# Encoder layer: the last K group of the first projection pass split in two, small loads placed behind the pass

## What is computed

```python
mod = silu(c) @ w_mod + b_mod            # 2048 -> 6 * 2048
sh1, sc1, gt1, sh2, sc2, gt2 = split(mod, 6)
h = x * (1 + sc1) + sh1
proj = h @ w_in                          # columns of four mixers: A (RWKV-7), B, C, D
y = concat(mixers(proj))
x = layer_norm(ALPHA * x + (1 + gt1) * (y @ w_out))
h = x * (1 + sc2) + sh2
gate, up = split(h @ w_up, 2)
x = layer_norm(ALPHA * x + (1 + gt2) * ((silu(causal_dwconv(gate)) * up) @ w_down))
```

## Time and profile before

| | us |
|---|---|
| median of 3 runs | 1441.3 (1440.76 to 1445.62) |
| profiled execution | 1437.06 |
| its span, first to last instruction | 1435.1 |
| PE busy | 1342.1 (94%) |
| DVE busy | 975.2 (68%) |
| ACT busy | 538.9 (38%) |
| POOL busy | 158.9 (11%) |
| DMA, mean over the span | 222 GB/s |

### The profile page before, as it was taken

The page is one execution under the profiler, slowest core; times in us unless marked ns, Lnnn a source line. Parts: engine busy times, 40 slices in busy tenths (PEclk is TensorE's granted clock), DMA queues, the critical chain, the costliest instruction groups (busy, mean ns, idle before and its releaser), DMA issues.

```text
span 1435.1 us, 23097 instructions
## 1 busy us (share of the span) xinstructions
PE 1342.1 (94%) x8833; PEld 1219.4 (85%) x8833; DVE 975.2 (68%) x1266; ACT 538.9 (38%) x765; POOL 158.9 (11%) x223
## 2 busy tenths in 40 slices
PE   1988899999999999997999999999999999999994
PEld 1777798989787777787999999999999998888883
DVE  5776787787779877568877787546555654545545
ACT  1000533343433435334544344434444453333331
POOL 4332111100001111001710100000000000000001
PEclk9899989999999999998999999999999999999997
...
DMA packets 142879, 318.98 MB, mean 222 GB/s; under 512 B 12142, under 2 KB 19680, under 8 KB 141792
## 3 DMA queue, kind: packets, MB, share of 16 engines
...
HBM read 315.98 MB, written 2.10 MB: 222 GB/s over the span
## 4 chain that ended last, share of the span: by engine, by line
PE 73%; DVE 14%; DMA 8%; issue 2%; ACT 2%; POOL 0%; DVEq 0%; POOLq 0%; ACTq 0%; SPq 0%
PE G L1377 64%; PE M L1377 8%; DMA MODA<-in_w_mod_dram 6%; DVE ACC L836 5%; DVE WLO L816 2%; DMA RAW<-in_w_out_dram 1%; DMA RAW<-in_w_in_dram 1%; ACT WHI L521 1%; DMA MODR<-in_w_mod_dram 1%; PE M L1538 0%; DVE X L1361 0%; DVE X L1370 0%; DVE SM L1125 0%; DVE HLO L868 0%; PE M L1640 0%
## 5 line engine op out<-in xcount | busy, mean ns | idle before, releaser
L1377 PE MATMUL G<-HHI,WHI 128*128 128x256 f32 (+1 forms) x1744 | 503.1, 288 | 0.0
L1377 PE MATMUL G<-HLO,WHI 128*128 128x256 f32 (+1 forms) x1744 | 495.4, 284 | 0.0
L1377 PE MATMUL G<-HHI,WLO 128*128 128x256 f32 (+1 forms) x1744 | 495.4, 284 | 0.0
L1377 PEld LDWEIGHTS G<-HHI,WHI 128*128 128x128 f32 (+1 forms) x1744 | 335.7, 192 | 4.2 <-issue 3.7
L1377 PEld LDWEIGHTS G<-HLO,WHI 128*128 128x128 f32 (+1 forms) x1744 | 335.8, 193 | 0.5 <-issue 0.5
L1377 PEld LDWEIGHTS G<-HHI,WLO 128*128 128x128 f32 (+1 forms) x1744 | 335.5, 192 | 0.0
L816 DVE TENSOR_TENSOR WLO<-RAW,WHI 128x1024 fp32r<-128x1024 f32 x182 | 221.3, 1223 | 167.4 <-ACT WHI L521 164.0
L821 DVE TENSOR_TENSOR WLO<-RAW,WHI 128x1024 fp32r<-128x1024 f32 x174 | 217.6, 1271 | 140.5 <-ACT WHI L527 140.3
L521 ACT ACTIVATE WHI<-RAW 128x1024 fp32r<-128x1024 f32 x182 | 191.9, 1059 | 209.9 <-PE G L1377 176.8
L527 ACT ACTIVATE WHI<-RAW 128x1024 fp32r<-128x1024 f32 x174 | 180.0, 1055 | 185.7 <-PE G L1377 138.0
L836 DVE SCALAR_TENSOR_TENSOR ACC<-MODR,SM,ACC 128x1024 f32<-128x1024 f32 x118 | 150.8, 1278 | 15.6 <-DMA MODR<-in_w_mod_dram 13.0
...
## 6 DMA issues: line engine op xcount, KB each, us to landing
RAW<-in_w_up_dram SPq DMA_DIRECT2D x176, 512.0 KB, 4.5
MODR<-in_w_mod_dram POOLq DMA_DIRECT2D x160, 512.0 KB, 5.6
RAW<-in_w_in_dram SPq DMA_DIRECT2D x88, 512.0 KB, 5.7
RAW<-in_w_down_dram SPq DMA_DIRECT2D x88, 512.0 KB, 4.3
MODA<-in_w_mod_dram POOLq DMA_DIRECT2D x32, 512.0 KB, 13.8
RAW<-in_w_out_dram SPq DMA_DIRECT2D x32, 512.0 KB, 4.5
...
```

What stands on the lines that cost most here:

```text
L1377: return pe.matmul(out_, l, r, start=start, stop=stop, skip_group_check=True)
```

## The change

- The last group (chunks 21 to 27, K tiles 12 to 15) is reordered: K, R and V chunks of tiles 12 and 13, then the LORA chunk of all four, then K, R, V of tiles 14 and 15. A LORA half waits only for the tiles of h that it reads.
- Its modulation, q = 48 to 63, comes in two half parts of 8 tiles: the first 8 hold the columns of K tiles 12 and 13, the others those of 14 and 15. A tile keeps its 512 KB but now has 2 rows of `w_mod` by 2 x 256 columns. It is loaded by two DMAs with rows of 1 KB (before: one DMA, rows of 2 KB), and added by two DVE instructions of 512 columns that wait for each other, instead of one of 1024.
- PE's column sums for the first half part (4 products) stand ahead of chunk 19, those of the second between the halves of chunk 22. Before, the 8 products stood ahead of chunk 21.
- The five small loads and `LNAB` stand between the loads of chunks 27 and 28.
- `DONE_IN` and `SETUP` follow: the LORA block is done first, then K, R, V. Tanh and sigmoid become a step "gates" of their own at place 26; squares, norms and the reciprocals stand 3 places later or more. Indices of semaphores move by one (`mod_sum`, `mod_col`).

```diff
@@ def chunk_at(n):
+    if g == GROUPS - 1:
+        return [(K_BLOCK, 12, 2), (R_BLOCK, 12, 2), (V_BLOCK, 12, 2), (LORA, 12, 4),
+                (K_BLOCK, 14, 2), (R_BLOCK, 14, 2), (V_BLOCK, 14, 2)][i]
...
-DONE_IN = {23: K_BLOCK, 24: LORA, 26: R_BLOCK, 28: V_BLOCK, 32: QI_BLOCK} | \
+DONE_IN = {25: LORA, 26: K_BLOCK, 27: R_BLOCK, 28: V_BLOCK, 32: QI_BLOCK} | \
...
+GROUP_AT = [(0, 0), (7, 0), (14, 0), (19, 0), (22, 1)]
+GROUP_KT = [(0, 4), (4, 8), (8, 12), (12, 14), (14, 16)]
+GROUP_MODS = [16, 32, 48, 56, 64]
...
-SETUP = {(23, 1): "squares", (24, 1): "norms", (25, 0): "inverse 0", (25, 1): "inverse 1", (26, 1): "inverse 2",
-         (27, 1): "inverse 3", (29, 1): "lora", (30, 1): "cumulate", (31, 1): "hats"}
+SETUP = {(26, 0): "gates", (26, 1): "squares", (27, 1): "norms", (28, 0): "inverse 0", (28, 1): "inverse 1", (29, 0): "inverse 2",
+         (30, 0): "inverse 3", (29, 1): "lora", (30, 1): "cumulate", (31, 1): "hats"}
@@ SP
-                if n == FIRST_CHUNKS + 3:
+                if n == WHOLE:
                     sp.dma_start(CBT[:, :], const_b.bitcast(bf16)).then_inc(late_in, 16)
...
-                if n == FIRST_CHUNKS + 5:
                     sp.wait_ge(h_lo, KT)
                     sp.dma_start(LNAB[:, :], rwkv_ln_b[0, :].partition_broadcast(P)).then_inc(lnab_in, 16)
@@ POOL
+                if m == 3:
+                    half, pair_ = divmod(t, KT // 2)
+                    c0 = m * 512 + half * 256
+                    for s_ in range(2):
+                        pool.dma_start(buf.rearrange("p (k s n) -> p k s n", k=2, s=2)[:, :, s_, :],
+                                       wm6[:, 2 * pair_:2 * pair_ + 2, s_, c0:c0 + 256]).then_inc(mod_in[s], 16)
+                    continue
@@ DVE, mod_add
+                if m == GROUPS - 1:
+                    half, pair_ = divmod(t, KT // 2)
+                    a = a[:, half * 512:half * 512 + 512]
+                    for k in range(2):
+                        ck, wk = CC[:, 2 * pair_ + k:2 * pair_ + k + 1], w[:, k * 512:k * 512 + 512]
+                        if pair_ == 0 and k == 0:
+                            mark(dve.tensor_scalar(a, wk, ck, None, ALU.mult))
+                            continue
+                        if k == 0:
+                            dve.wait_ge(mod_done, q)
+                        else:
+                            settle()
+                        ins = dve.scalar_tensor_tensor(a, wk, ck, a, ALU.mult, ALU.add)
+                        mark(ins) if k == 0 else ins.then_inc(mod_done, 1)
+                    return
@@ DVE, the groups
-            for g in range(GROUPS):
-                mod_add(g + 1, 0)
+            for g, kts in enumerate(GROUP_KT):
+                q = GROUP_MODS[g]
+                mod_add(*divmod(q, KT))
                 mod_cols(g)
                 dve.wait_ge(mod_col, g + 1)
-                for kt in range(4 * g, 4 * g + 4):
+                for kt in range(*kts):
                     h_new_tile(kt)
...
@@ PE
+                    q0 = 4 if GROUP_MODS[g] % KT == 0 and g == len(GROUP_KT) - 1 else 0
+                    mod_reduce(min(g, GROUPS - 1), range(q0, q0 + 2 * (GROUP_KT[g][1] - GROUP_KT[g][0])))
...
+                if n < WHOLE and (half == 0 or kts == 4):
+                    pe.wait_ge(h_new, kt + (kts if kts == 2 else 2 * half + 2))
...
-                if n <= FIRST_CHUNKS and n % GROUP_CHUNKS == 0:
-                    first_parts((n // GROUP_CHUNKS,))
                 for half in range(2):
+                    if (n, half) in GROUP_AT:
+                        first_parts((GROUP_AT.index((n, half)),))
                     w_in_half(n, half)
```

More of the change, by code:

```diff
@@ L44 @@
 MODS_IN = (MOD_PARTS - 2) * KT
-MOD_LAPS = 4 * KT // FIRST_RING + (MODS_IN - 4 * KT) // RING
+MOD_LAPS = 5 * KT // FIRST_RING + (MODS_IN - 4 * KT) // RING
 UP_MODS = 4
@@ L578, in setup @@
             def setup(what):
-                if what == "lora":
+                if what == "gates":
                     act.wait_ge(evac_lora, 2)
@@ L583, in setup @@
                     act.activation(PA[:, 13, :], PA[:, 13, :], ACT.Sigmoid)
+                elif what == "lora":
                     act.wait_ge(lora_pe, 2)
@@ L829, in mod_add @@
                 a, ck = ACC[:, m % 2, :], CC[:, t:t + 1]
+                if t == 0 and m >= 2:
+                    dve.wait_ge(mod_sum, m - 1 if m <= GROUPS else m)
+                if m == GROUPS - 1:
[13 more added lines that the diff above has]
+                    return
                 if t == 0:
-                    if m >= 2:
-                        dve.wait_ge(mod_sum, m - 1)
                     ins = dve.tensor_scalar(a, w, ck, None, ALU.mult)
@@ L839, in mod_cols @@
             def mod_cols(m):
-                dve.wait_ge(mod_sum, m + 1)
-                if m < GROUPS:
-                    two = lambda a: a[:, 0:32].rearrange("p (s k) -> p s k", s=2)[:, :, 4 * m:4 * m + 4]
-                    dve.tensor_tensor(two(MC), M[3][:, 0:8].rearrange("p (s k) -> p s k", s=2), two(BMC), ALU.add)\
+                if m < len(GROUP_KT):
+                    k0, k1 = GROUP_KT[m]
+                    dve.wait_ge(mod_sum, m + 1)
+                    two = lambda a: a[:, 0:32].rearrange("p (s k) -> p s k", s=2)[:, :, k0:k1]
+                    dve.tensor_tensor(two(MC), M[3][:, 0:2 * (k1 - k0)].rearrange("p (s k) -> p s k", s=2), two(BMC), ALU.add)\
                        .then_inc(mod_col, 1)
                     return
+                m -= 1
+                dve.wait_ge(mod_sum, m + 2)
                 at = slice(8 * m + 16, 8 * m + 24)
@@ L876, in h_new_tile @@
                                   MC[:, SH1 + kt:SH1 + kt + 1], ALU.mult, ALU.add).then_inc(h_new, 1)
-            for g in range(GROUPS):
-                mod_add(g + 1, 0)
+            for g, kts in enumerate(GROUP_KT):
+                q = GROUP_MODS[g]
+                mod_add(*divmod(q, KT))
                 mod_cols(g)
                 dve.wait_ge(mod_col, g + 1)
-                for kt in range(4 * g, 4 * g + 4):
+                for kt in range(*kts):
                     h_new_tile(kt)
-                mod_add(g + 1, 1)
-                for kt in range(4 * g, 4 * g + 4):
+                mod_add(*divmod(q + 1, KT))
+                for kt in range(*kts):
                     h_split(kt, 0)
-                if g == 0:
-                    for n in range(AHEAD):
-                        split_lo(n)
-                if g < GROUPS - 1:
-                    for t in range(MODS_BESIDE_H, KT):
-                        mod_add(g + 1, t)
-                        if t % 2:
-                            split_lo(g * GROUP_CHUNKS + t // 2 - 1 + AHEAD)
+                if g + 1 < len(GROUP_KT):
+                    for q in range(q + MODS_BESIDE_H, GROUP_MODS[g + 1]):
+                        mod_add(*divmod(q, KT))
             def evac_in(b):
@@ L1167, in _ @@
                     if last_turn is not None:
-                        mod_cols(last_turn)
+                        mod_cols(last_turn + 1)
                     last_turn = turns.get((n, half))
@@ L1397, in tm, with mod_reduce @@
                 return ins
-            def mod_reduce(m):
-                for q in range(8):
-                    ins = mm(M[3][:, q:q + 1], ACC[:, m % 2, q * P:(q + 1) * P], ONES[:, 0:1],
+            def mod_reduce(m, qs=range(8)):
+                for q in qs:
+                    ins = mm(M[3][:, q - qs[0]:q - qs[0] + 1], ACC[:, m % 2, q * P:(q + 1) * P], ONES[:, 0:1],
                              start=True, stop=True)
@@ L1420, in first_parts @@
             def first_parts(ms):
-                for m in ms:
-                    pe.wait_ge(mod_done, (m + 1) * KT)
-                    if m:
-                        pe.wait_ge(mod_col, m)
-                    mod_reduce(m)
+                for g in ms:
+                    pe.wait_ge(mod_done, GROUP_MODS[g])
+                    if g:
+                        pe.wait_ge(mod_col, g)
+                    q0 = 4 if GROUP_MODS[g] % KT == 0 and g == len(GROUP_KT) - 1 else 0
+                    mod_reduce(min(g, GROUPS - 1), range(q0, q0 + 2 * (GROUP_KT[g][1] - GROUP_KT[g][0])))
             def w_in_half(n, half):
@@ L1487, in setup @@
                 elif what == "norms":
-                    pe.wait_ge(mod_col, 4)
+                    pe.wait_ge(mod_col, len(GROUP_KT))
                     pe.wait_ge(evac_lora, 2)
```

12 lines of the change are left out of this document (6 added, 6 removed).

## The result

The change takes 1448.1 us (median of 20 runs, 1443.37 to 1456.24), the kernel before 1442.7 us (median of 20, beside them): a ratio of 1.0037, 95% interval 1.0021 to 1.0053, or **+3.0 to +7.6 us, 5.4 in the middle**. That is measurably slower, and under the 0.5% that the prediction took as its bound. One of the twenty executions of the kernel before took 6478 us and is left out of the ratio and its interval. 1448.9 was predicted, with 1440 to 1455 as the range. The profiled execution of the change took 1447.8 us (span 1445.9); that of before took 1437.06 (span 1435.1), 5.6 us under the median of its own 20 runs, so the difference of these two spans (10.8 us) is twice that of the medians. In what follows the traces give places and causes, and the ratios give the time.

A forecast was written before the change was run, and what follows sets the result against it. Up to about 159 us arriving weights and modulation were the bound, then DVE until "gram". 2.9 + 4.3 + 0.4 = +7.6 us on 1437.06 gave 1444.7; with the median 4.2 above, 1448.9, range 1440 to 1455.

The forecast's parts named there:

- The first pass: PE up to chunk 24: no stall worth counting, chunk 24 ends at 145.4, chunk 28 issued 7 us earlier.
- Chunk 28's landing: SP's queue: chunk 28 waits behind the small loads, lands at 161 (151.2 to 165.5); DVE splits it 2.9 us later.
- Behind the split: DVE from chunk 28's split to "gram": moved work adds 4.3 us, R's evacuation waiting for ACT adds 0.4.
- From "gram" to the end: After "gram" PE is the bound again and carries the +7.6 us to the end as it is.
- Rows of 1 KB: Loads of tiles 48 to 63: 12% more engine time per MB, 2.6 us, covered, so nothing booked.
- In time: Rival, chance 0.22: chunk 28 lands by 157 as DVE's additions stall for their tiles; -2.2 to +3 us.
- Starved modulation: Rival, chance 0.15: narrow rows cut POOL's share per queue turn, last tile lands at 134 to 136; +9 to +13 us.
- PE sets the pace: Rival, chance 0.08: "gram" waits for PE, DVE's work can come later; needs chunk 28 by 152; -8 us.
- the prize: PE in the first pass, around chunks 19 to 22: 5.1 us of idle time and 2.2 us of low clock.
- the moved work: K's evacuation, two norm steps and one reciprocal, now behind DVE's split of chunk 28: +4.3 us.

The follow-up runs named there:

- e2: The change with all six small loads ahead of chunk 32, behind the loads of 28 to 31; ratio to the kernel before 0.9993.
- e7: The kernel before with modulation tiles 48 to 63 loaded by two DMAs each with rows of 1 KB; ratio to the kernel before 1.0018.

## Why the prediction was right, and where not

The mechanism was right: the first pass gained what was forecast, chunk 28 queued behind the small loads, and DVE passed the delay on to "gram". That 1448.9 lies within 0.8 us of the measured 1448.1 is partly luck, as two errors of the sum made up for each other.

- **The first pass: right.** Chunk 24 was to end at 145.4 and ended at 145.0, chunk 28's issue was to come at 145.8 and came at 145.52. PE had no idle time over 0.4 us between 103 and 155 us. 1.54 us for a tile in two additions (1.5 estimated) and 1.05 us for the half sums (1.0) were right.
- **Chunk 28's landing: right in its cause, 1.7 us short.** 161 predicted, 162.7 measured. Two things were mis-sized. From 141.9 to 162.7 us SP's queue moved 4.00 MB, where I had 3.1 (I had counted a rest of 0.1 MB and nothing of the chunks issued behind 28; but chunk 26, 0.52 MB, issued at 138.18, landed only 8.0 us later), and POOL's 3.65 (3.9). And the rate was not the earlier trace rows's 0.388 MB per us throughout, but 0.367 on the whole, with the slump of the last section in it. The change's queues in that stretch (packets, MB, share of 16 engines), and its windows around the slump (columns of the earlier trace rows):

```profile
q1 hardware_dynamic: 2416, 4.00, 55.7%
q0 software_dynamic: 1005, 3.65, 48.5%
```

```profile
146.00:148.00 2.00, 2.00 (x11) 1.77 (x10) 1.08 (x2) 0.00 (x0) 0.53 (x1) 1.00 1.02 410
...
150.00:152.00 2.00, 2.00 (x11) 1.75 (x10) 0.61 (x1) 0.00 (x0) 0.11 (x1) 1.00 1.02 318
```

- **Behind the split: right in its cause, 1.5 us too much.** 4.3 + 0.4 was booked, 3.2 measured: DVE is busy 3.6 us longer there (four reciprocals instead of three, K's evacuation and the norm steps, with 14 additions at 17.5 us instead of 17.8), has 0.4 us less idle time, and R's evacuation waits only 0.2. The two errors made up for each other: the sum was 7.6 at "gram" and the trace shows 7.8. In e2 this step takes 4.5 us. The early tanh and sigmoid save one table load, not two: sigmoid's table is loaded again for the gates, at 176.49 in the change; DVE does not show it.
- **From "gram" to the end: open.** The prediction carried the 7.6 us on as they were, above a median of 1441.3; the measured difference is 5.4 (3.0 to 7.6). Before's trace is of an execution 5.6 us under its median. From "gram" to the first step on `GTR` (L1016 in the kernel before, near 300 us) the traces of the twelve experiments take between 91.9 and 98.4 us, before 92.4 and the change 94.0, with no relation to an edit that I could find: one trace places a mechanism, and does not size an effect of 5 us.
- **Rows of 1 KB: about right.** 2.6 us on the tiles, covered in the change, was the estimate; e7 uncovers them and costs 2.6 us (0.9 to 4.3). The 12% of engine time per MB was a little high: POOL's queue took 63.5% of the engines for 4.84 MB before and 69.5% for 4.87 MB in e7, 9% more. By the Trainium skill ("DMA: Bandwidth & Descriptors", Specifications), 512 B are enough for the full rate, which would have made e7 equal to before; the windows (361 against 385 GB/s) disagree, unless it is the double number of transfers that costs.
- **The rivals.** *In time* (0.22) fell: chunk 28 landed at 162.7, with the additions of tiles 66 to 70 waiting 0.28 to 1.66 us each, as it said, but without freeing enough. *Starved modulation* (0.15) fell: in 110 to 130 us of the change POOL's queue moved 4.56 MB and SP's 2.68 with 1390 packets each, in e7 4.87 and 2.34. e7's 1483 packets of POOL carry 3.3 KB each, three narrow rows, where before's 1336 carry 3.6, so that narrow rows hardly change POOL's bytes per turn. By the Trainium skill ("DMA: Bandwidth & Descriptors", Queues, rings and completion order) a turn is a packet of several descriptors. Three rows of 1 KB to a packet fit that; whether the turns go by packets, these counts leave open (1390 each in the change, but 1336 and 1603 before). *PE sets the pace* (0.08) fell in the change and, more tellingly, in e2, where its condition (chunk 28 early) nearly held: split at 153.70, yet "gram" at 200.25, DVE busy for 43.64 of 45.46 us.
- **What the sum did not say.** It counted the prize and the moved work in one line, so that the loss looked like one of queueing. e2 shows that with the queueing at chunk 28 taken away the change only comes back to the time of the kernel before.
